# Probabilities times V as one float32 product with the turned probabilities loaded

## The chip, the cores and the metric

The kernel runs on one core of a Trainium2 chip. The metric is the device time of one launch in microseconds (us), the median of several runs. TensorE is written PE below (PEld is its weight load), VectorE is DVE, ScalarE is ACT, GpSimd is POOL and SyncE is SP.

## The reference

One step of a one-layer streaming encoder over 1024 prompt rows and 64 sample rows of width 1024, all in float32:

```
h = rms_norm(x) @ W_in                      # q, k, v of four mixers A, B, C, D, four heads of 64 each
A: stick-breaking weights  w = sigmoid(z) * prod(1 - sigmoid(z of later keys)),   out = w @ v
B: softmax over the own chunk and 2 chunks before, with a sink and a bias,        out = p @ v
C: p = softmax(q1 k1) - lam * softmax(q2 k2), two products with 32 dimensions,    out = rms_norm(p @ v)
D: softmax over the own chunk and 8 chunks before, with a bias,                   out = p @ v
x = x + concat(A, B, C, D) @ W_out
x = x + (silu(rms_norm(x) @ W_gate) * (rms_norm(x) @ W_up)) @ W_down
y = rms_norm(x)                             # and the K and V rows are outputs too
```

The change concerns the four products with v.

## The kernel before

The kernel has three large parts: the projection (up to about 320 us of the profile), the attention (about 325 to 863 us) and the output projection with the feed-forward part (the rest). Float32 products are made as three products of float32r operands: each operand is split into a rounded high part and a low part, and `split_product` (L677 to L679) adds high by high, high by low and low by high in PSUM. In the attention ACT makes the high parts and DVE or POOL the low ones.

The attention runs in rounds, one job each. A job is one score matrix: mixer, block of 128 queries (nine per head, the last one the 64 sample rows) and head; C has two jobs for each block and head. The jobs of one output make a unit: 180 jobs, 144 units, in the order A, B, C, D. The keys of a unit are cut into 1 to 8 blocks of 128, 512 blocks over all units (44 of them with the 64 sample queries). Round r of the loop has, on each engine in this order (all engines run it in parallel, tied by semaphores):

- PE: the scores of job r; `turn_value` of the unit that is 4 rounds old (L846); `turn_probs` of the unit 2 rounds old, one transpose of 128x128 a key block, up to four into one PSUM bank (L813); `values` of the unit 3 rounds old; after the fourth head of a block `turn_out` (L855), which brings the output rows into the layout of the next product.
- ACT: the high parts of q, k and v in the first rounds of a mixer (`high_v`, L1038); the copy of the output of `values` from PSUM to `oT_one` (L1053); the exponential or sigmoid (L1019, L1012); the copies of the turned probabilities to `pt_hi` (L1065).
- DVE: the low parts of v (L1290; for C they are on POOL, L1520) and of q and k; the row maximum (L1234, L1237) or A's scan along the keys (L1248); C's joining of its two matrices (`combine`, L1258); the low parts of the turned probabilities `pt_lo` (L1311); the scaled output rows (`output`, L1272, L1275, L1280).
- POOL: masks and differences of A (L1487, L1495), reciprocals (L1540, L1545), C's split and C's output variance.

`values` multiplies, for each key block, V (64 columns, loaded as the weights) with the turned probabilities (128 queries, streaming), three products a block. Its result is the output turned round, 64x128. So ACT copies it to SBUF, and `turn_value` turns it back on PE before DVE reads it. V must be split before that: each V part's low half takes the place of V in SBUF, so that a mixer's split waits until V has been stored to DRAM (`vrow_out`) and the cached V is in (`vcache_in`).

PE's banks 4 and 5 hold the turned probabilities (and `turn_out`'s result); they come free by `batch_copied`, which DVE raises when the low part is made. Banks 6 and 7 hold the output of `values`.

Of the kernel before, what the change touches and what calls it, by code (L numbers as in the profile page):

```python
# [23 lines left out]
P = 128  # L24
# [73 lines left out]
def build(nc, x_prompt, x_sample, cache_a, cache_b, cache_c, cache_d, norm_attn_g, w_in, w_out,  # L98
# [34 lines left out]
    p_index = {n: i for i, n in enumerate(p_batches)}  # L133

    with ExitStack() as ctx:
# [46 lines left out]
        v_rows_r = sb("v_rows_r", [P, NT, KV_W], F32R, r1r)  # L182
        v_cache_r = sb("v_cache_r", [P, 2, KV_W], F32R, r1r)
# [45 lines left out]
        v_hi = sb("v_hi", [P, NT + 2, 256], F32R, p3)  # L229
        o_rows = sb("o_rows", [P, 2, 256], F32, p3)  # L230
        probs_e = sb("probs_e", [P, 2, D_MODEL], F32, p3)
        oT_one = sb("oT_one", [64, 2, P], F32, p3)
# [23 lines left out]
        pt_hi = [hT_r[:, 14 + s, 0:D_MODEL].rearrange("p (b q) -> p b q", q=P) for s in range(2)]  # L256
        pt_lo = [hT_r[:, 20 + s, 0:D_MODEL].rearrange("p (b q) -> p b q", q=P) for s in range(2)]
# [61 lines left out]
        pt_hi_ready = sem("pt_hi_ready")  # L319
        batch_copied = sem("batch_copied")  # L320
        qk_hi_ready = sem("qk_hi_ready")
        qk_split = sem("qk_split")
        v_hi_ready = sem("v_hi_ready")
        v_split = sem("v_split")
        pv_done = sem("pv_done")
        oT_copied = sem("oT_copied")
        oT_turned = sem("oT_turned")
# [137 lines left out]
        def v_parts(m):  # L465

            w, at = width[m], ROW_OFF[m]
            old = slice(1, 2) if m == "B" else slice(0, 2)
            new = [(v_rows[:, x:y, at:at + w], v_hi[:, x:y, 0:w], v_rows_r[:, x:y, at:at + w])
                   for x, y in ((0, EARLY_BLOCKS), (EARLY_BLOCKS, 5), (5, NT - 1))]  # L470
            return new + [
                    (v_rows[0:DEC, NT - 1, at:at + w], v_hi[0:DEC, NT - 1, 0:w], v_rows_r[0:DEC, NT - 1, at:at + w]),
                    (v_cache[:, old, at:at + w], v_hi[:, NT + old.start:NT + 2, 0:w], v_cache_r[:, old, at:at + w])]

# [12 lines left out]
        V_PARTS, V_EARLY = 5, 1  # L487
        V_ROUND = 2
        def splits_at(r):

            out = []
            for m in "ABCD":
                k = r - first_job[m]
                if k == 0:
                    out.append(("qk", m, 0, QK_EARLY))
                if 1 <= k <= QK_PARTS - QK_EARLY:
                    out.append(("qk", m, QK_EARLY + k - 1, QK_EARLY + k))
                k -= V_ROUND + 1
                if k == 0:
                    out.append(("v", m, 0, V_EARLY))  # L500
                k -= 2
                if 1 <= k <= V_PARTS - V_EARLY:
                    out.append(("v", m, V_EARLY + k - 1, V_EARLY + k))
            return out
# [24 lines left out]
        a_jobs = sum(job.mixer == "A" for job in jobs)  # L529

# [143 lines left out]
        def _(pe):  # L674
# [143 lines left out]
            def values(u):  # L818
# [8 lines left out]
                v_h = slice(job.v_col - ROW_OFF[job.mixer], job.v_col - ROW_OFF[job.mixer] + 64)  # L827
                for t in range(job.blocks):
                    w = job.key_width(t)
                    if t % 4 == 0:  # L830
                        pe.wait_ge(batch_copied, batches[("p", u, t // 4)] + 1)
                    if job.i != SAMPLE:
                        high, low = v_hi[:, job.first + t, v_h], v_rows_r[:, job.first + t, v]
                    elif t < job.past:
                        high, low = v_hi[:, NT + job.first + t, v_h], v_cache_r[:, job.first + t, v]
                    else:
                        high, low = v_hi[0:w, NT - 1, v_h], v_rows_r[0:w, NT - 1, v]
                    mm = split_product(bank(6 + u % 2, job.rows, 64), high, low, pt_hi[u % 2][0:w, t, 0:job.rows],
                                       pt_lo[u % 2][0:w, t, 0:job.rows], t == 0, t == job.blocks - 1)
                mm.then_inc(pv_done, 1)  # L840

            def turn_value(u):

                n = units[u][0].rows
                pe.wait_ge(oT_copied, u + 1)
                pe.transpose(bank(6 + u % 2, 64, n, 256), oT_one[:, u % 2, 0:n], ident[0:64, 0:64])\  # L846
                    .then_inc(oT_turned, 1)

            def turn_out(u):
# [3 lines left out]
                pe.wait_ge(batch_copied, n - 1)  # L853
# [6 lines left out]
            for r in range(rounds):  # L860
                if r < NJ:
                    scores(jobs[r])
                if unit_at(r - NORM_LAG) is not None:
                    turn_value(unit_at(r - NORM_LAG))
# [87 lines left out]
        def _(act):  # L952
# [91 lines left out]
            for r in range(rounds):  # L1044
                for kind, m, at, to in splits_at(r):
                    (high_qk if kind == "qk" else high_v)(m, at, to)
                u = unit_at(r - NORM_LAG)
                if u is not None:
                    n = units[u][0].rows
                    act.wait_ge(pv_done, u + 1)  # L1050
                    if u >= 2:
                        act.wait_ge(oT_turned, u - 1)
                    act.copy(oT_one[:, u % 2, 0:n], bank(6 + u % 2, n, 64)).then_inc(oT_copied, 1)  # L1053
# [5 lines left out]
                if u is not None:  # L1059
                    for b in range(-(-units[u][0].blocks // 4)):  # L1060
# [3 lines left out]
                        for src, to in batch_parts(u, b):  # L1064
                            ins = act.copy(pt_hi[u % 2][to], src)  # L1065
                        ins.then_inc(pt_hi_ready, 1)
                u = unit_at(r - NORM_LAG)
                if u is not None and units[u][0].mixer == "C":
# [3 lines left out]
                    act.wait_ge(oT_turned, u + 1)  # L1072
# [3 lines left out]
                    act.activation(hT[0:n, 9, D_MODEL:D_MODEL + 64], bank(6 + u % 2, 64, n, 256), ACT.Square,  # L1076
# [5 lines left out]
            act.wait_ge(batch_copied, len(batches))  # L1082
# [45 lines left out]
        def _(dve):  # L1128
# [132 lines left out]
            def output(u):  # L1261
# [5 lines left out]
                src = bank(6 + u % 2, 64, n, 256)  # L1267
                if job.head == 0 and u >= 8:
                    dve.wait_ge(batch_ready, batches[("o", u - 5)] + 1)
                if job.mixer == "A":  # L1270
                    dve.wait_ge(oT_turned, u + 1)
# [5 lines left out]
                else:  # L1277
                    dve.wait_ge(inv_ready, inv_count[u])
                    dve.wait_ge(oT_turned, u + 1)
# [151 lines left out]
        def _(pool):  # L1431
# [91 lines left out]
            for u, unit in enumerate(units):  # L1523
                while next_round <= unit[-1].n + 1:
                    for kind, m, at, to in splits_at(next_round):
                        if on_pool(m, at):
                            low_half(kind, m, at)
# [80 lines left out]
```

## Time and profile before

| | us |
|---|---|
| median of 3 runs | 1783.87 |
| the runs | 1776.14, 1783.87, 1784.74 |
| span of the profiled execution | 1776.3 |
| attention in it | about 325 to 863 |

The profile is one execution, and its own time is the span of 1776.3 us between the first and the last instruction; nothing else lies around it. It is as short as the fastest of the three runs and is 7.6 us below their median. "Busy" is the share of time in which an engine has an instruction in hand. PEclk is the granted TensorE clock: 1.00 stands for 2.4 GHz and 0.50 for 1.2 GHz. The ends of matmuls are modelled, since they are pipelined, so how fast PE works is read from one start to the next.

### The profile page before, as it was taken

How to read it: one execution, taken by the hardware profiler on the slowest of the kernel's cores; microseconds unless marked ns; L12 is line 12 of the kernel's file. 1: busy time of each engine (PE TensorE's matmuls, PEld its weight loads, DVE VectorE, ACT ScalarE, POOL GpSimd, SP SyncE). 2: the span in 40 equal slices, each digit the busy share in tenths (PEclk: the TensorE clock that was granted, in tenths of full speed). 3: DMA queues.
4: the chain of work that ended last, by engine and by line, in shares of the span. 5: the costliest groups of instructions: out<-in, count | busy, mean ns of one | idle time of the engine just before them, and what ended most of it. 6: DMA issues, size and time to landing. Idle time of an engine off the chain costs nothing.

```text
span 1776.3 us, 25708 instructions
## 1 busy us (share of the span) xinstructions
PE 1693.1 (95%) x9689; PEld 1511.5 (85%) x9689; DVE 826.3 (47%) x1617; ACT 456.9 (26%) x1160; POOL 259.8 (15%) x437
## 2 busy tenths in 40 slices
PE   5999999799987999999799999999999999999997
PEld 4999999687865777778687899999999999999996
DVE  6111111678665555667722542442543524425425
ACT  4211112545564433455612101001000010010002
POOL 7000000245245322331022100000000000000001
PEclk9999999679575555659899999999999999999999
DMA  7111110400000000010120410111111101111002
GB/s 226 37 47 35 47 47 15 151 1 2 1 1 1 1 0 1 1 72 2 67 82 1 142 48 25 47 47 47 47 44 50 47 24 47 47 47 47 0 0 112
DMA packets 90737, 75.88 MB, mean 43 GB/s; under 512 B 5928, under 2 KB 83273, under 8 KB 90653
## 3 DMA queue, kind: packets, MB, share of 16 engines
q1 hardware_dynamic: 90668, 75.01, 13.7%
q8 instruction: 39, 0.64, 0.1%
q14 instruction: 30, 0.24, 0.0%
HBM read 64.06 MB, written 10.77 MB: 42 GB/s over the span
## 4 chain that ended last, share of the span: by engine, by line
PE 89%; DVE 4%; POOL 3%; ACT 1%; issue 1%; DMA 1%; SPq 1%; ACTq 0%; POOLq 0%; DVEq 0%
PE acc L677 28%; PE acc L678 26%; PE acc L679 26%; PE acc L813 5%; PE acc L846 1%; POOL xlo L1460 1%; PE acc L855 1%; PE acc L759 1%; PE acc L927 1%; PE acc L692 1%; DVE hT_r L1335 1%; DVE hT_r L1311 0%; DVE hT L1248 0%; DVE hT L1258 0%; DMA hT<-in_x_prompt_dram 0%
## 5 line engine op out<-in xcount | busy, mean ns | idle before, releaser
L677 PE MATMUL acc<-ohi,gu_hi 128*128 128x384 f32 (+1 forms) x1056 | 344.3, 326 | 2.8 <-DVE gu_lo L1159 1.9
L679 PE MATMUL acc<-ohi,gu_lo 128*128 128x384 f32 (+1 forms) x1056 | 344.2, 326 | 0.0
L678 PE MATMUL acc<-olo,gu_hi 128*128 128x384 f32 (+1 forms) x1056 | 344.0, 326 | 0.0
L677 PEld LDWEIGHTS acc<-ohi,gu_hi 128*128 128x128 f32 x1056 | 198.2, 188 | 3.8 <-issue 3.3
L678 PEld LDWEIGHTS acc<-olo,gu_hi 128*128 128x128 f32 x1056 | 198.2, 188 | 0.4
L679 PEld LDWEIGHTS acc<-ohi,gu_lo 128*128 128x128 f32 x1056 | 198.2, 188 | 0.0
L1107 ACT ACTIVATE silu<-acc 128x384 f32<-128x384 f32 (+1 forms) x66 | 31.3, 474 | 639.7 <-PE acc L679 638.6
L1384 DVE TENSOR_TENSOR prod<-acc,silu 128x384 f32<-128x384 f32 (+1 forms) x66 | 35.3, 535 | 336.7 <-ACT silu L1107 336.7
L677 PE MATMUL acc<-xhi,win_hi 128*128 128x384 f32 (+1 forms) x528 | 173.1, 328 | 0.0
L679 PE MATMUL acc<-xhi,win_lo 128*128 128x384 f32 (+1 forms) x528 | 172.5, 327 | 0.0
L678 PE MATMUL acc<-xlo,win_hi 128*128 128x384 f32 (+1 forms) x528 | 172.5, 327 | 0.0
L1404 DVE TENSOR_TENSOR x<-acc,x 128x512 f32<-128x512 f32 x198 | 134.4, 689 | 69.1 <-PE acc L679 64.4
L677 PE MATMUL acc<-hT_r,v_hi 128*64 128x128 f32 (+1 forms) x512 | 139.3, 289 | 5.3 <-DVE v_rows_r L1290 2.7
L677 PE MATMUL acc<-k_hi,q_hi 32*128 32x512 f32 (+12 forms) x264 | 129.4, 492 | 12.3 <-DVE hT_r L1285 9.2
L679 PE MATMUL acc<-dn_hi,h_lo 128*128 128x512 f32 x352 | 137.1, 389 | 0.0
L678 PE MATMUL acc<-dn_lo,h_hi 128*128 128x512 f32 x352 | 137.0, 389 | 0.0
L677 PE MATMUL acc<-dn_hi,h_hi 128*128 128x512 f32 x352 | 137.0, 389 | 0.0
L1451 POOL TENSOR_SCALAR meansq<-sumsq 128x1 f32<-128x1 f32 (+1 forms) x27 | 8.9, 329 | 858.4 <-ACT sq_junk L955 767.0
L678 PE MATMUL acc<-hT_r,v_hi 128*64 128x128 f32 (+1 forms) x512 | 126.8, 264 | 0.0
L679 PE MATMUL acc<-hT_r,v_rows_r 128*64 128x128 f32 (+1 forms) x484 | 119.2, 263 | 0.0
L1311 DVE TENSOR_TENSOR hT_r<-acc,hT_r 128x512 fp32r<-128x512 f32 (+4 forms) x208 | 91.8, 466 | 58.2 <-ACT hT_r L1065 57.6
L1065 ACT CAST hT_r<-acc 128x512 fp32r<-128x512 f32 (+4 forms) x208 | 79.3, 412 | 132.5 <-PE acc L813 131.8
(179 smaller groups left out, 3121.4 us busy)
## 6 DMA issues: line engine op xcount, KB each, us to landing
win_raw<-in_w_in_dram SPq DMA_DIRECT2D x22, 512.0 KB, 3.9
ffn_raw<-in_w_gate_dram SPq DMA_DIRECT2D x22, 512.0 KB, 3.8
ffn_raw<-in_w_up_dram SPq DMA_DIRECT2D x22, 512.0 KB, 4.4
ffn_raw<-in_w_down_dram SPq DMA_DIRECT2D x22, 512.0 KB, 4.1
hT<-in_x_prompt_dram SPq DMA_DIRECT2D x8, 512.0 KB, 7.0
hT<-in_w_out_dram SPq DMA_DIRECT2D x8, 512.0 KB, 5.0
x<-in_x_prompt_dram SPq DMA_DIRECT2D x8, 512.0 KB, 5.9
out_dram<-y_out SPq DMA_DIRECT2D x8, 512.0 KB, 2.6
```

Source lines behind the costliest of these rows:

```text
L677: pe.matmul(out, a_hi, b_hi, start=first, stop=False)
L678: pe.matmul(out, a_hi, b_lo, start=False, stop=False)
L679: return pe.matmul(out, a_lo, b_hi, start=False, stop=last)
L692: mm = pe.transpose(bank(base + t % 4, n, at=q * P), xs(j)[0:n, d * P:(d + 1) * P], ident[0:n, 0:n])
L759: mm = pe.transpose(bank(n % 4, P, rows_of(j), t * P), hT[:, tile, j * P:j * P + rows_of(j)], ident[:])
L813: mm = pe.transpose(bank(4 + n % 2, job.rows, w, (t % 4) * P), prob_slot[job.n % 4][0:job.rows, t * P:t * P + w], ident[0:job.rows, 0:job. ...
L846: pe.transpose(bank(6 + u % 2, 64, n, 256), oT_one[:, u % 2, 0:n], ident[0:64, 0:64])\
L1065: ins = act.copy(pt_hi[u % 2][to], src)
L1107: act.activation(silu[:, q % 2, 0:n], bank(2 * (q % 2), n), ACT.Silu).then_inc(silu_done, 1)
L1311: ins = dve.tensor_tensor(pt_lo[u % 2][to], src, pt_hi[u % 2][to].bitcast(F32), ALU.subtract)
L1384: dve.tensor_tensor(prod[:, q % 2, 0:n], bank(2 * (q % 2) + 1, n), silu[:, q % 2, 0:n], ALU.mult).then_inc(prod_done, 1)
L1404: dve.tensor_tensor(part, bank(4 + m % 4), part, ALU.add).then_inc(y_added, 1)
```

## The change

V is no longer split, and the turned probabilities are no longer split. For each key block one float32 product takes their place in which the turned probabilities (128 keys by 128 queries) are the loaded operand and V (64 columns) streams. Its result has queries on the partitions, so the copy to `oT_one` and `turn_value` fall away. Banks 4 and 5 come free when ACT has copied (`pt_copied`), or, after `turn_out`, when DVE has (`o_copied`). SBUF keeps its layout by placeholders. ACT waits at the end of the attention for V's stores; PE waits for the cached V once, at A's sample block.

```diff
-        v_rows_r = sb("v_rows_r", [P, NT, KV_W], F32R, r1r)
-        v_cache_r = sb("v_cache_r", [P, 2, KV_W], F32R, r1r)
+        sb("over_v_rows", [P, NT, KV_W], F32, r1r)
+        sb("over_v_cache", [P, 2, KV_W], F32, r1r)
...
-        pt_hi = [hT_r[:, 14 + s, 0:D_MODEL].rearrange("p (b q) -> p b q", q=P) for s in range(2)]
-        pt_lo = [hT_r[:, 20 + s, 0:D_MODEL].rearrange("p (b q) -> p b q", q=P) for s in range(2)]
+        probs_t = [hT[:, 14 + s, 0:D_MODEL].rearrange("p (b q) -> p b q", q=P) for s in range(2)]
...
+        def wait_batch(eng, n):
+            if n in p_index:
+                eng.wait_ge(pt_copied, p_index[n] + 1)
+            else:
+                eng.wait_ge(o_copied, o_index[n] + 1)
...
             def turn_probs(u):
-                        pe.wait_ge(batch_copied, n - 1)
+                        wait_batch(pe, n - 2)
...
             def values(u):
-                if u == first_unit[job.mixer]:
-                    pe.wait_ge(v_split, V_PARTS * "ABCD".index(job.mixer) + V_EARLY)
-                if job.i >= EARLY_BLOCKS and job.head == 0:
-                    pe.wait_ge(v_split, V_PARTS * ("ABCD".index(job.mixer) + 1))
+                if job.i == SAMPLE and job.head == 0 and job.mixer == "A":
+                    pe.wait_ge(vcache_in, 16 * N_CACHE)
...
-                        pe.wait_ge(batch_copied, batches[("p", u, t // 4)] + 1)
+                        pe.wait_ge(pt_copied, p_index[batches[("p", u, t // 4)]] + 1)
...
-                    mm = split_product(bank(6 + u % 2, job.rows, 64), high, low, pt_hi[u % 2][0:w, t, 0:job.rows],
-                                       pt_lo[u % 2][0:w, t, 0:job.rows], t == 0, t == job.blocks - 1)
+                    mm = pe.matmul(bank(6 + u % 2, 64, job.rows), probs_t[u % 2][0:w, t, 0:job.rows], rows,
+                                   start=t == 0, stop=t == job.blocks - 1)
                 mm.then_inc(pv_done, 1)
-            def turn_value(u):
-                n = units[u][0].rows
-                pe.wait_ge(oT_copied, u + 1)
-                pe.transpose(bank(6 + u % 2, 64, n, 256), oT_one[:, u % 2, 0:n], ident[0:64, 0:64])\
-                    .then_inc(oT_turned, 1)
...
-            def high_v(m, at, to):
-                if at == 0:
-                    if m != "A":
-                        act.wait_ge(pv_done, first_unit[m])
-                    act.wait_ge(vrow_out[m], 16 * sum(kv_target(m, j) is not None for j in range(NT)))
-                    act.wait_ge(vcache_in, 16 * N_CACHE)
-                for src, high, _ in v_parts(m)[at:to]:
-                    act.copy(high, src).then_inc(v_hi_ready, 1)
...
-                    act.copy(oT_one[:, u % 2, 0:n], bank(6 + u % 2, n, 64)).then_inc(oT_copied, 1)
...
-                            ins = act.copy(pt_hi[u % 2][to], src)
-                        ins.then_inc(pt_hi_ready, 1)
+                            ins = act.copy(probs_t[u % 2][to], src)
+                        ins.then_inc(pt_copied, 1)
...
-                    act.wait_ge(oT_turned, u + 1)
+                    act.wait_ge(pv_done, u + 1)
...
-            act.wait_ge(batch_copied, len(batches))
+            act.wait_ge(o_copied, len(o_batches))
+            for m in "ABCD":
+                act.wait_ge(vrow_out[m], 16 * sum(kv_target(m, j) is not None for j in range(NT)))
...
-                src = bank(6 + u % 2, 64, n, 256)
+                src = bank(6 + u % 2, 64, n)
...
-            def low_v(m, at, to):
-                for i, (src, high, low) in enumerate(v_parts(m)[at:to], at):
-                    dve.wait_ge(v_hi_ready, V_PARTS * "ABCD".index(m) + i + 1)
-                    dve.tensor_tensor(low, src, high.bitcast(F32), ALU.subtract).then_inc(v_split, 1)
...
-                    for b in range(-(-units[u][0].blocks // 4)):
-                        dve.wait_ge(pt_hi_ready, p_index[batches[("p", u, b)]] + 1)
-                        for src, to in batch_parts(u, b):
-                            ins = dve.tensor_tensor(pt_lo[u % 2][to], src, pt_hi[u % 2][to].bitcast(F32), ALU.subtract)
-                        ins.then_inc(batch_copied, 1)
```

## Rows read from the trace of the kernel before

**Rows 1.** The page: engines, and the granted clock in 40 slices.
```profile
PE 1693.1 (95%) x9689; PEld 1511.5 (85%) x9689; DVE 826.3 (47%) x1617; ACT 456.9 (26%) x1160; POOL 259.8 (15%) x437
...
PEclk9999999679575555659899999999999999999999
```

**Rows 2.** The page: the chain that ended last, by engine.
```profile
PE 89%; DVE 4%; POOL 3%; ACT 1%; issue 1%; DMA 1%; SPq 1%; ACTq 0%; POOLq 0%; DVEq 0%
```

**Rows 3.** Windows: stretch, length, PE, PEld, DVE, ACT, POOL busy, PEclk.
```profile
325.80:377.00 51.20, 45.03 (x209) 35.64 (x210) 31.92 (x60) 23.99 (x58) 17.94 (x33) 0.50 0.25 74
377.00:441.80 64.80, 60.66 (x597) 52.69 (x595) 58.76 (x82) 35.09 (x79) 37.11 (x38) 1.00 0.00 1
441.80:493.10 51.30, 50.02 (x271) 41.60 (x271) 33.64 (x131) 28.22 (x99) 13.01 (x22) 0.50 0.01 1
...
545.00:687.60 142.60, 140.39 (x577) 104.17 (x577) 80.08 (x205) 57.62 (x184) 42.40 (x111) 0.50 0.00 1
687.60:757.00 69.40, 64.97 (x372) 51.02 (x372) 45.89 (x104) 33.17 (x95) 19.45 (x50) 0.65 0.00 1
...
800.20:858.30 58.10, 55.89 (x546) 49.32 (x546) 43.56 (x143) 35.25 (x104) 11.49 (x21) 1.00 0.01 2
```

**Rows 4.** The page: the costliest groups, first product with V.
```profile
L677 PE MATMUL acc<-hT_r,v_hi 128*64 128x128 f32 (+1 forms) x512 | 139.3, 289 | 5.3 <-DVE v_rows_r L1290 2.7
```

**Rows 5.** Windows: instructions with v_hi alone (two products a block).
```profile
377.00:441.80 64.80, 24.17 (x230) 21.81 (x230) 0.00 (x0) 0.00 (x0) 0.00 (x0) 1.00 0.00 1
...
800.20:858.30 58.10, 21.58 (x196) 18.88 (x196) 0.00 (x0) 0.00 (x0) 0.00 (x0) 1.00 0.01 2
```

**Rows 6.** Windows: instructions with oT_one alone (PE, PEld, ACT).
```profile
377.00:441.80 64.80, 4.53 (x18) 2.45 (x18) 4.88 (x19) 1.00 0.00 1
...
800.20:858.30 58.10, 5.54 (x22) 2.94 (x22) 5.61 (x22) 1.00 0.01 2
```

**Rows 7.** Timeline of PE (start, duration) at 1.2 GHz: V, 12 steps apart.
```profile
641.64 0.31 PE L679 MATMUL acc<-hT_r,v_rows_r 128*64 128x128 f32 x1
...
642.92 0.31 PE L679 MATMUL acc<-hT_r,v_rows_r 128*64 128x128 f32 x1
```

**Rows 8.** Timeline of PE at 2.4 GHz: V, 16 steps apart.
```profile
399.58 0.23 PE L678 MATMUL acc<-hT_r,v_hi 128*64 128x128 f32 x1
...
400.54 0.22 PE L679 MATMUL acc<-hT_r,v_rows_r 128*64 128x128 f32 x1
```

**Rows 9.** Timeline of PE at 1.2 GHz: scores, 128 columns loaded, 128 streaming.
```profile
522.01 0.41 PE L678 MATMUL acc<-hT_r,q_hi 32*128 32x128 f32 x1
522.23 0.41 PE L679 MATMUL acc<-k_hi,hT_r 32*128 32x128 f32 x1
```

**Rows 10.** Source line L729, true float32 products: durations, first and last start.
```profile
L729 PE MATMUL acc<-hT x12: 590/592/592, 62.7 to 67.4; 128*128 128x512 f32 x12
```

**Rows 11.** Timeline of PE at 1.2 GHz: turn_value, transposes behind it.
```profile
645.37 0.36 PE L846 MATMUL acc<-ident,oT_one 64*128 64x64 f32 x1
645.67 1.54 PE L813 MATMUL acc<-ident,hT 128*128 128x128 f32 x6
```

**Rows 12.** Waits, 325 to 377 us: total, times, longest.
```profile
PE acc L677 <- DVE v_rows_r L1290: 2.7, 1, 2.7
```

**Rows 13.** Waits, 515 to 545 us.
```profile
PE acc L813 <- DVE hT L1258: 7.1, 2, 4.5
```

**Rows 14.** Timeline of POOL: a split of C's V (two of this size).
```profile
533.39 1.81 POOL L1520 TENSOR_TENSOR v_rows_r<-v_rows,v_hi 128x768 fp32r<-128x768 f32 x1
```

**Rows 15.** Windows: DVE's line L1311 alone.
```profile
377.00:441.80 64.80, 18.71 (x37) 1.00 0.00 1
```

**Rows 16.** Windows in C: before and in a spell at 2.4 GHz.
```profile
684.20:687.60 3.40, 3.40 (x26) 2.75 (x24) 1.66 (x4) 0.22 (x2) 1.17 (x3) 0.50 0.02 5
687.60:691.00 3.40, 3.40 (x18) 2.55 (x18) 3.14 (x6) 2.00 (x6) 0.00 (x0) 1.00 0.00 0
```

**Rows 17.** Windows: instructions with v_hi alone, before that spell.
```profile
684.20:687.60 3.40, 2.40 (x14) 2.21 (x14) 0.00 (x0) 0.00 (x0) 0.00 (x0) 0.50 0.02 5
```

More of the change, by code:

```diff
@@ L133, in build @@
     p_index = {n: i for i, n in enumerate(p_batches)}
+    o_batches = [n for key, n in sorted(batches.items(), key=lambda kv: kv[1]) if key[0] == "o"]
+    o_index = {n: i for i, n in enumerate(o_batches)}
     with ExitStack() as ctx:
@@ L494, in splits_at @@
                 if k == 0:
-                    out.append(("qk", m, 0, QK_EARLY))
+                    out.append((m, 0, QK_EARLY))
                 if 1 <= k <= QK_PARTS - QK_EARLY:
[L497 to L503, printed above, removed]
+                    out.append((m, QK_EARLY + k - 1, QK_EARLY + k))
             return out
@@ L830, in values @@
                     if t % 4 == 0:
-                        pe.wait_ge(batch_copied, batches[("p", u, t // 4)] + 1)
[L832 to L835, printed above, removed]
-                    else:
-                        high, low = v_hi[0:w, NT - 1, v_h], v_rows_r[0:w, NT - 1, v]
-                    mm = split_product(bank(6 + u % 2, job.rows, 64), high, low, pt_hi[u % 2][0:w, t, 0:job.rows],
-                                       pt_lo[u % 2][0:w, t, 0:job.rows], t == 0, t == job.blocks - 1)
+                        pe.wait_ge(pt_copied, p_index[batches[("p", u, t // 4)]] + 1)
+                    if job.i == SAMPLE and t < job.past:
+                        rows = v_cache[0:w, job.first + t, v]
+                    elif job.i == SAMPLE:
+                        rows = v_rows[0:w, NT - 1, v]
+                    else:
+                        rows = v_rows[0:w, job.first + t, v]
+                    mm = pe.matmul(bank(6 + u % 2, 64, job.rows), probs_t[u % 2][0:w, t, 0:job.rows], rows,
+                                   start=t == 0, stop=t == job.blocks - 1)
                 mm.then_inc(pv_done, 1)
-            def turn_value(u):
-                n = units[u][0].rows
-                pe.wait_ge(oT_copied, u + 1)
-                pe.transpose(bank(6 + u % 2, 64, n, 256), oT_one[:, u % 2, 0:n], ident[0:64, 0:64])\
-                    .then_inc(oT_turned, 1)
             def turn_out(u):
@@ L1044, in _ @@
             for r in range(rounds):
[L1045 to L1052, printed above, removed]
-                    act.copy(oT_one[:, u % 2, 0:n], bank(6 + u % 2, n, 64)).then_inc(oT_copied, 1)
+                for m, at, to in splits_at(r):
+                    high_qk(m, at, to)
                 if r < NJ and jobs[r].mixer == "A":
@@ L1075, in _ @@
                         act.wait_ge(c_factor, k)
-                    act.activation(hT[0:n, 9, D_MODEL:D_MODEL + 64], bank(6 + u % 2, 64, n, 256), ACT.Square,
+                    act.activation(hT[0:n, 9, D_MODEL:D_MODEL + 64], bank(6 + u % 2, 64, n), ACT.Square,
                                    scale=row_inv[0:n, job.n:job.n + 1], accum_out=c_var[0:n, 1:2])\
@@ L1510, in output_root, with low_qk @@
                     .then_inc(c_factor, 1)
-            def low_half(kind, m, part):
-                parts, per_mixer, ready, done = ((qk_parts(m), QK_PARTS, qk_hi_ready, qk_split) if kind == "qk"
-                                                 else (v_parts(m), V_PARTS, v_hi_ready, v_split))
-                src, high, low = parts[part]
-                count = per_mixer * "ABCD".index(m) + part
-                pool.wait_ge(done, count)
-                pool.wait_ge(ready, count + 1)
-                pool.tensor_tensor(low, src, high.bitcast(F32), ALU.subtract).then_inc(done, 1)
+            def low_qk(m, part):
+                src, high, low = qk_parts(m)[part]
+                count = QK_PARTS * "ABCD".index(m) + part
+                pool.wait_ge(qk_split, count)
+                pool.wait_ge(qk_hi_ready, count + 1)
+                pool.tensor_tensor(low, src, high.bitcast(F32), ALU.subtract).then_inc(qk_split, 1)
             next_round = 0
@@ L1524, in _ @@
                 while next_round <= unit[-1].n + 1:
-                    for kind, m, at, to in splits_at(next_round):
+                    for m, at, to in splits_at(next_round):
                         if on_pool(m, at):
-                            low_half(kind, m, at)
+                            low_qk(m, at)
                     next_round += 1
```

37 lines of the change are left out of this document (8 added, 29 removed).

## The prediction

> **What bounds the kernel now.** The page comes first: PE is busy for 95% of the span, and 89% of the chain that ended last is PE [rows 1, 2]. The change leaves the projection and the feed-forward part alone, so I cut the attention into stretches wherever the granted clock changes and read the busy times there [rows 3]. The reader is to see two kinds of stretch. At 1.2 GHz PE has nearly no pause: 140.4 of 142.6 us in C, 50.0 of 51.3 in B. There one step of PE more is one step of time more. At 2.4 GHz (A from 377 to 441.8, D from 800.2 to 858.3) PE is busy too, but in A DVE is busy for 58.8 of 64.8 us and the two wait for each other. The page's PEclk digits of 5 to 7 say that most of the attention runs at 1.2 GHz [rows 1]. What follows is therefore costed at either level, by the step from one start to the next, because durations of pipelined matmuls overlap.
>
> **Products with V.** Each of the 512 blocks [rows 4] now has three instructions, each loading 64 columns and streaming 128. Twelve steps take 1.28 us at 1.2 GHz, 0.107 each, so a block costs 0.32 us [rows 7]; at 2.4 GHz sixteen take 0.96, 0.060 each, 0.18 us a block [rows 8].
>
> The new product is true float32. The bias flips are such products: six in the code are 12 instructions in the trace, each 0.427 us after the last ((67.4 - 62.7)/11) for 512 streaming columns at 2.4 GHz [rows 10]. That is two instructions a product, and each column streams twice. So a new block is two instructions, each loading 128 columns and streaming 64. Streaming takes twice 64 columns, 0.107 us at 1.2 GHz. Loading is longer: where 128 columns are loaded for 128 that stream, the step is 0.22 us, twice the 0.107 that streaming them needs [rows 9]. I take exactly twice, 0.213. A block is then 2 x 0.213 = 0.427 us at 1.2 GHz and half of that, 0.214, at 2.4: 0.107 and 0.034 us more than now. This takes it that a load lies wholly behind the product before it, as in [rows 9]. If it didn't, an instruction would cost 0.213 + 0.107 and a block 0.64; if the load cost nothing, a block would be 0.214. I take 0.427, since the row has the same load size.
>
> The Trainium skill, page "TensorE: Matmul & The Clock Gate", section "LDWEIGHTS (loading the stationary operand)", gives a load as its columns divided by 1.2 in ns, which is 0.107 us for 128 columns at either clock. By that a new block would cost 0.214 at 1.2 GHz and the change would save about 0.1 us on each block there. The row says 0.213 a load, and the row decides.
>
> How many at which clock: at two instructions a block [rows 5], 115 blocks in A's fast stretch and 98 in D's run at 2.4 GHz; I put the other 299 at 1.2 (some in B and C are faster, at a price near the same). Of the 512, 44 have 64 queries; loading 64 columns only, they gain about 0.107 us each at 1.2 GHz instead, and 32 of them are there. Sum: 267 x 0.107 - 32 x 0.107 = +25 us, and at 2.4 GHz 201 x 0.034, less 12 x 0.05, = +6. Together **+31 us**.
>
> **The second turn.** `turn_value` takes 0.30 us of PE at 1.2 GHz before the transposes behind it can start [rows 11], and half of that at 2.4. 40 of 144 are in the fast stretches [rows 6]. Removed: 104 x 0.30 + 40 x 0.15 = 37 us. Seven of the slow ones lie between 513 and 545 us, where PE stands waiting anyway, so **-35 us**. The ACT copies to `oT_one` (4.9 us in A's stretch) go as well; ACT has room everywhere (35.1 of 64.8), so that is worth nothing by itself.
>
> So PE's own work changes by -4 us: the turn pays for the loads.
>
> **Waits that go.** At A's start the first product waits 2.7 us for V's low part [rows 12], and the high part before it was held back by the cached V and V's stores; without them PE starts its values as soon as they are turned: -4. At C's start PE waits 7.1 us for DVE's joining [rows 13]; that waits for POOL's reciprocals, and in POOL's queue between them stand the splits of V, two of 1.8 us and two shorter ones [rows 14]. The splits of q and k stay there and take the same places, so I count -4, the two of 1.8, and not the whole 7. In A's fast stretch DVE loses L1311, 18.7 of its 58.8 us [rows 15], and is no longer close to the bound; PE is, at 61 of 65. I count -4, from the few pauses it has. In the slow stretches L1311 and V's splits are hidden behind PE now, and dropping them yields nothing. The bank of the turned probabilities comes free one DVE instruction sooner, which shortens nothing PE waits for in C. New waits: PE waits once for the cached V at A's last block, which A's first product with V already waits for now, so it is free. ACT waits for V's stores after the last product; SP stored them hundreds of us before. Total of the waits **-12**.
>
> With the clock as it is: 1776.3 - 16 = 1760 for the profiled execution, and 1783.9 - 16 = 1768 for the median, of which the profiled span is 7.6 us short.
>
> **The clock.** This is the large unknown. In C PE is at 1.2 GHz although it pauses for only 2.2 of 142.6 us [rows 3]. Its first rise follows a stretch that products with V fill for 2.4 of 3.4 us, and lasts for the next stretch, without such products [rows 16, 17]. From 687.6 to 757 the mean clock is 0.65 [rows 3], so (0.65 - 0.50)/0.50 x 69.4, about 20 us of it, are at 2.4 GHz in a few spells of this kind. The new product leaves the array streaming for only half of its time, the load taking the rest; so I expect some of these spells to go. All of them gone: 20 us of work at half the speed, less the quarter in which PE paused, +15. I take half, **+8**.
>
> **Forecast:** 1783.9 - 16 + 8 = **1776 us**, its own range 1760 to 1792 (all or none of the spells, and 8 for the waits). Chance 0.55.
>
> **Rivals.**
>
> *The clock of A, B and D falls too* (slower). What speaks for it: C shows that PE without pause can stay at 1.2, and half of A's products with full use of the array go. Against: A's fast stretch holds over 65 us, also where DVE holds PE up. Price: in A's fast stretch a unit has 6.5 blocks on average; at 1.2 GHz its scores are 832 x 3 columns, 2.1 us, transposes 6.5 x 0.213 = 1.4, products 6.5 x 0.427 = 2.8, and 0.4 between them: 6.7 us, for 18 units 120 us against 64.8. D's 20 units of 5 blocks at 5.6 us make 111 against 58. With B's 20 us it is +115: 1768 + 115 = 1883, or 1898 with C's spells gone. It decides from about a tenth of those stretches on. Chance 0.27, most of it between 1820 and 1898, since one stretch can fall alone.
>
> *The clock rises in C* (much faster). PE's pauses shorten, which speaks for it; C staying at 1.2 with next to none speaks against. At 2.4 GHz PE's 140 us become 70, and then DVE's 80 less its lows (about 16) and the chain of ACT and DVE would bound: about 87, -55, and -10 in the rest of C: 1703. The page named above lays a low clock to pauses between bursts of matmuls (section "Why this matters for your kernels"); by that rule the clock would be kept or rise. The stretches of C do not agree with it [rows 3]. Chance 0.10.
>
> *Loads are not hidden:* 0.64 us a block, +0.32 x 267 + 0.14 x 201 = +113, less the 35 and 12 above and a few for the 64-query blocks: 1784 + 113 - 47 = about 1850. The row of the loads speaks against [rows 9]. Chance 0.05. Other ways 0.03.
>
> **How the numbers follow.** The measurement can tell about 0.5% from no change, 1775 to 1793. Of the forecast's 0.55, 0.26 ends below, 0.25 within and 0.04 above; the rise in C adds 0.10 below, and the other cases, 0.35, are above. So faster 0.36, same 0.25, slower 0.39. The range leaves out the far end of the fall (over 1885, 0.10) and most of the rise in C (under 1755, 0.10): 1755 to 1885.
>
> **What would show it.** Right: products with V as 1024 instructions, 0.21 us apart at 1.2 GHz and 0.107 at 2.4; no L846; A's PEclk 1.00 from about 375 us; DVE at 40 of A's 60 us. Wrong: steps of 0.32 (loads in the open) or 0.11 (loads cheaper than in rows 9, -50 us); PEclk 0.50 all through A or D; C at 1.00 anywhere for longer than 10 us; and a wait of PE on ACT's copy of the turned probabilities at C's start as long as the 7.1 before.

## The result, and the profile after

The changed kernel takes 1895.5 us (median of 4 runs, 1886.0 to 1896.6), the kernel before 1784.1 beside it (4 runs, 1776.1 to 1784.7): ratio 1.064, interval 1.059 to 1.069. It is slower by 111 us; the forecast said 1776 and 1755 to 1885. The price of the first rival, 1883 to 1898, is what was measured. Some executions run a few per cent longer at a lower granted clock; ratios and intervals here leave those out, medians and ranges don't.

The page of the profile after (engines, the granted clock in 40 slices, the chain that ended last by engine) answers to [rows 1, 2]:

```profile
span 1893.5 us, 23855 instructions
PE 1826.1 (96%) x9033; PEld 1632.6 (86%) x9033; DVE 744.7 (39%) x1393; ACT 417.2 (22%) x996; POOL 249.3 (13%) x433
...
PEclk8999999555555555555559999999999999999999
...
PE 92%; POOL 3%; DVE 2%; issue 1%; ACT 1%; DMA 1%; SPq 0%; ACTq 0%; POOLq 0%; DVEq 0%
```

PE has 656 instructions fewer than before and is busy 133 us longer. The digits tell why: slices 8 to 21 are all 5, where before there were 6, 7, 8 and 9 among them. The records of the clock say the same: from 324.0 to 993.0 us, all through the attention, the granted clock is 0.50, 1.2 GHz. The windows of the attention stretches, with the same columns as [rows 3], show that PE doesn't pause more than before (over the attention it is busy for 628.9 of 652 us, before for 497.4 of 534):

```profile
377.00:441.80 64.80, 64.80 (x245) 56.23 (x244) 32.66 (x23) 17.24 (x31) 18.33 (x21) 0.50 0.00 1
441.80:530.00 88.20, 86.20 (x370) 74.41 (x369) 39.43 (x99) 32.54 (x88) 24.07 (x33) 0.50 0.00 1
530.00:800.00 270.00, 257.75 (x894) 200.56 (x892) 113.85 (x332) 98.37 (x302) 77.82 (x175) 0.50 0.00 1
800.00:960.00 160.00, 155.50 (x619) 133.03 (x620) 55.64 (x189) 54.81 (x162) 30.67 (x63) 0.50 0.05 20
```

From 377 us on, where PE had gone over to 2.4 GHz in [rows 3], it is now busy for all of 64.8 us at 1.2 GHz.

Cut at the first exponential or sigmoid of each mixer, and at D's last exponential, which can be found in both traces:

| stretch | before, us | of it at 2.4 GHz | after, us | of it at 2.4 GHz | difference |
|---|---|---|---|---|---|
| A | 119.8 | 64.9 | 169.6 | 0 | +49.8 |
| B | 70.5 | 20.5 | 82.4 | 0 | +11.8 |
| C | 241.1 | 20.5 | 253.0 | 0 | +11.9 |
| D | 98.2 | 56.3 | 143.5 | 0 | +45.3 |

That is 118.8 us; the spans (1893.5 and 1776.3) are 117.2 apart, the rest of the kernel being 1.6 shorter. What the change did to the work can be read where both kernels run at 1.2 GHz: from A's job 0 to job 16, and from C's job 72 to job 124. Windows of these stretches, before (the first two) and after:

```profile
517.20:687.50 170.30, 155.58 (x640) 115.25 (x639) 92.30 (x238) 69.41 (x227) 62.88 (x134) 0.50 0.00 1
326.90:372.80 45.90, 39.96 (x182) 31.30 (x181) 29.82 (x55) 21.67 (x54) 16.65 (x31) 0.50 0.25 76
```
```profile
578.30:744.30 166.00, 155.25 (x510) 118.22 (x509) 72.06 (x201) 61.14 (x195) 57.19 (x130) 0.50 0.00 1
326.40:370.60 44.20, 40.09 (x141) 31.48 (x142) 25.45 (x36) 15.98 (x37) 17.06 (x31) 0.50 0.27 78
```

170.3 us became 166.0 and 45.9 became 44.2. At an equal clock the work got a little cheaper, as forecast, so the loss is put down to the clock; the experiments test that.

### The profile page after: what moved, and what is told of

The parts are those of the page before. It is cut to its first block, busy times and chain, and to the rows that moved or that the text cites. A ratio compares the mean times of both kernels' runs of the same rounds, so it can differ in the third digit from the quotient of the medians.

```text
span 1893.5 us, 23855 instructions
## 1 busy us (share of the span) xinstructions
PE 1826.1 (96%) x9033; PEld 1632.6 (86%) x9033; DVE 744.7 (39%) x1393; ACT 417.2 (22%) x996; POOL 249.3 (13%) x433
## 4 chain that ended last, share of the span: by engine, by line
PE 92%; POOL 3%; DVE 2%; issue 1%; ACT 1%; DMA 1%; SPq 0%; ACTq 0%; POOLq 0%; DVEq 0%
PE acc L659 25%; PE acc L661 23%; PE acc L660 23%; PE acc L817 11%; PE acc L795 7%; PE acc L827 1%; POOL xlo L1404 1%; PE acc L897 1%; PE acc L674 0%; DVE hT_r L1279 0%; PE acc L741 0%; DVE hT_r L1241 0%; POOL c_var L1449 0%; DVE olo L1275 0%; DMA hT<-in_x_prompt_dram 0%
## 5 line engine op out<-in xcount | busy, mean ns | idle before, releaser
L817 PEld LDWEIGHTS acc<-v_rows,hT 128*128 128x128 f32 (+1 forms) x968 | 218.1, 327 | 15.2 <-issue 6.6
L817 PE MATMUL acc<-v_rows,hT 128*128 128x64 f32 (+1 forms) x968 | 225.8, 410 | 1.2 <-DVE o_rows L1231 1.2
L659 PE MATMUL acc<-k_hi,q_hi 32*128 32x512 f32 (+12 forms) x264 | 149.8, 569 | 10.2 <-DVE hT_r L1241 7.8
L1019 ACT COPY hT<-acc 128x512 f32<-128x512 f32 (+4 forms) x208 | 80.3, 410 | 250.5 <-PE acc L795 249.6
L661 PE MATMUL acc<-k_hi,hT_r 32*128 32x512 f32 (+12 forms) x264 | 127.4, 486 | 0.0
L659 PEld LDWEIGHTS acc<-k_hi,q_hi 64*128 64x128 f32 (+3 forms) x264 | 74.2, 282 | 51.0 <-issue 23.7
```

The lines of the kernel that those rows point to most:

```text
L659: pe.matmul(out, a_hi, b_hi, start=first, stop=False)
L661: return pe.matmul(out, a_lo, b_hi, start=False, stop=last)
L817: mm = pe.matmul(bank(6 + u % 2, 64, job.rows), probs_t[u % 2][0:w, t, 0:job.rows], rows, start=t == 0, stop=t == job.blocks - 1)
L1019: ins = act.copy(probs_t[u % 2][to], src)
```

## The experiments

The theory: the products with V now stream 64 columns for every 128 loaded, and that takes the clock from PE. The rivals: something else of the change costs the time (the instructions' number, the removed turn, waits), or the clock falls only because PE has less or more to do. The kernel before was run again beside each group of experiments (medians 1784.7 to 1800.8 us), and each ratio is to those runs.

**V streams 128 columns.** The neighbouring head's V streams along and its result is not read.

```diff
-                v = slice(job.v_col, job.v_col + 64)
+                v = slice(job.v_col - 64 * (job.v_col // 64 % 2), job.v_col - 64 * (job.v_col // 64 % 2) + 128)
...
-                    mm = pe.matmul(bank(6 + u % 2, 64, job.rows), probs_t[u % 2][0:w, t, 0:job.rows], rows,
+                    mm = pe.matmul(bank(6 + u % 2, 128, job.rows), probs_t[u % 2][0:w, t, 0:job.rows], rows,
```

> The changed kernel with V streaming 128 columns instead of 64 for each loaded block of probabilities; the 64 columns of the neighbouring head are computed and not used. Streaming 128 columns twice takes 0.213 us at 1.2 GHz, as long as the load of 128 columns, so that PE's work at an equal clock stays what it is. Theory (the 111 us are the clock: the same work at 1.2 GHz, because the loads leave the array without streaming columns): A and D go back to 2.4 GHz for most of their time, steps of 0.107 us there, 1760 to 1790 us. Rival 1 (loading the probabilities, or a wait of the new order, costs the time): no change, 1890 to 1900, or more if streaming adds to the load. Rival 2 (the clock falls because of float32 products or of the missing turn, not of idle columns): PEclk stays 0.50, 1890 to 1900.

Measured: 1756.0 us (1753.8 to 1761.3), ratio to before 0.984, interval 0.974 to 0.993. The trace has the same 23855 instructions as the changed kernel. The timeline of PE at 1.2 GHz, first the changed kernel, then this one:

```profile
705.79 2.82 PE L817 MATMUL acc<-v_rows,hT 128*128 128x64 f32 x12
```
```profile
564.84 2.08 PE L817 MATMUL acc<-v_rows,hT 128*128 128x128 f32 x8
```

A row is the time from the first start to the last end. A last instruction in it takes 0.42 us in both, so the steps are at most (2.82 - 0.42)/11 = 0.22 and (2.08 - 0.42)/7 = 0.24, with a longer first one in each row; the median from one start to the next is 0.213 us in both kernels. The columns that were added are free at 1.2 GHz, as forecast from the load of 128 columns, which sets the step. With the same steps at the same clock the kernel is 139 us faster, and its windows show where from:

```profile
358.00:436.60 78.60, 75.95 (x538) 64.82 (x538) 65.00 (x61) 35.31 (x71) 39.70 (x46) 1.00 0.00 1
436.60:457.00 20.40, 20.40 (x79) 15.05 (x79) 11.85 (x47) 10.95 (x34) 7.14 (x10) 0.50 0.00 1
457.00:498.00 41.00, 39.41 (x277) 31.56 (x275) 23.88 (x119) 26.49 (x92) 14.88 (x28) 1.00 0.01 1
503.00:638.00 135.00, 126.14 (x403) 94.08 (x404) 59.62 (x170) 49.27 (x161) 46.47 (x111) 0.50 0.00 1
...
778.00:839.00 61.00, 60.18 (x440) 52.21 (x440) 29.06 (x106) 30.98 (x82) 10.93 (x20) 1.00 0.01 1
```

A, B and D are at 2.4 GHz again (78.5, 40.6 and 56.3 us), A and B for longer than before the change and D for as long. So neither the removed turn nor the waits cost anything; this version keeps all of the change but the width of what streams.

**The old roles in float32.** V is loaded (64 columns), the turned probabilities stream (128 columns), and the copy to `oT_one` and `turn_value` are back; V and the probabilities stay unsplit.

```diff
-                    mm = pe.matmul(bank(6 + u % 2, 64, job.rows), probs_t[u % 2][0:w, t, 0:job.rows], rows,
+                    mm = pe.matmul(bank(6 + u % 2, job.rows, 64), rows, probs_t[u % 2][0:w, t, 0:job.rows],
...
+            def turn_value(u):
+                pe.wait_ge(oT_copied, u + 1)
+                pe.transpose(bank(6 + u % 2, 64, n, 256), oT_one[:, u % 2, 0:n], ident[0:64, 0:64])\
+                    .then_inc(oT_turned, 1)
...
```

> The changed kernel with the roles of before: V is loaded (64 columns), the turned probabilities stream (128), still one float32 product and no splits; the copy to oT_one and turn_value are back. A block is two instructions of 128 columns streamed twice, 0.427 us at 1.2 GHz, as in the changed kernel; the turn adds 0.30 a unit, 35 us in all. Theory (clock, through columns that don't stream): A and D at 2.4 GHz again, 1784 + 31 for the products - 12 for the waits = about 1803, less if C rises too. Rival (work): 1895 + 35 = 1930.

Measured: 1802.0 us (1791.9 to 1813.1), ratio 1.008, interval 1.003 to 1.014. A was at 2.4 GHz for 81.9 us, C for 51.2, D for 57.6. True float32 as such doesn't take the clock; loading the wide operand and streaming the narrow one does.

**Halves.** Each product is made of two, with 64 queries each: 64 columns loaded, 64 streaming.

```diff
-                    mm = pe.matmul(bank(6 + u % 2, 64, job.rows), probs_t[u % 2][0:w, t, 0:job.rows], rows,
-                                   start=t == 0, stop=t == job.blocks - 1)
+                    for q in range(0, job.rows, 64):
+                        out = acc[q:q + 64, (6 + u % 2) * 512:(6 + u % 2) * 512 + 64]
+                        mm = pe.matmul(out, probs_t[u % 2][0:w, t, q:q + 64], rows,
+                                       start=t == 0, stop=t == job.blocks - 1)
```

> The changed kernel with each block's product cut into two of 64 queries: four instructions, each loading 64 columns (0.107 us at 1.2 GHz) and streaming V's 64 twice (0.107), 0.427 a block as now. Theory (clock): the array streams all the time with 64 of its 128 columns; if streaming time is what counts, A and D are back at 2.4 GHz and it takes 1760 to 1790; if only half of the array's columns doesn't do, 1890 to 1900 with PEclk 0.50. Rival (work): 1895, and above it if the 64-column steps are longer than 0.107.

Measured: 1789.9 us (1773.1 to 1804.2), ratio 1.000, interval 0.995 to 1.006. This looks like the clock brought back, but it isn't the test that I meant it to be, since the work didn't stay the same. The expectation had 0.427 us a block; the trace shows two blocks of 128 queries, eight instructions, in one row at 1.2 GHz:

```profile
562.54 0.69 PE L819 MATMUL acc<-v_rows,hT 128*64 128x64 f32 x8
```

An instruction alone is 0.31 us long. The two products of a block write to different halves of the partitions; they start 0.007 us apart, and the next pairs follow 0.107 us apart, so the two run beside each other. A block costs about 0.21 us, half of what it costs in the changed kernel. C shows it without the clock: at 1.2 GHz throughout in both profiled executions, it takes 227.7 us where it took 253.0. By an estimate from these steps (0.213 us less in each of 468 blocks of 128 queries), up to 100 of the 106 us can be cheaper work. With less work than the kernel with 128 columns it is still slower (its fastest execution took 1773.1 us, that kernel's longest 1761.3), so it keeps less of the clock; how much it keeps isn't shown.

**Filler.** Two extra products a unit, 4 columns loaded and 128 streaming, whose result is overwritten. If streaming anything often enough kept the clock, this would.

```diff
+                for k in range(2):
+                    pe.matmul(bank(6 + u % 2, P, 4, 256), ident[:, 0:4], ident[:], start=True, stop=True)
```

> The changed kernel with two products more in each of the 144 units, whose result nobody reads: 4 columns of the identity loaded, its 128 streaming, float32, 0.85 us a unit at 1.2 GHz and 0.43 at 2.4. Theory (clock): more work, yet A and D rise to 2.4 GHz: 1895 - 95 + 31 there and + 61 in B and C, about 1890. Rival (work): 1895 + 144 x 0.85 = 2017.

Measured: 2016.8 us (2008.7 to 2017.3), ratio 1.127, interval 1.116 to 1.138: what the rival had said, 2017. The extra work was paid in full and more (a unit's four instructions take 0.95 us at 1.2 GHz, not 0.85), and only 37.7 us of the attention, in A, ran at 2.4 GHz. My theory missed here as I had put it: streaming alone isn't enough. PE was busy throughout, too, and without the clock:

```profile
350.00:466.00 116.00, 116.00 (x420) 84.17 (x420) 48.02 (x45) 26.82 (x48) 27.64 (x38) 0.50 0.00 1
504.40:630.00 125.60, 125.05 (x492) 80.15 (x492) 36.22 (x163) 35.13 (x124) 22.34 (x37) 0.50 0.00 1
```

**Filler with 128 columns loaded.** The same two products a unit with the whole of `ident` loaded instead of 4 columns of it.

```diff
-                    pe.matmul(bank(6 + u % 2, P, 4, 256), ident[:, 0:4], ident[:], start=True, stop=True)
+                    pe.matmul(bank(6 + u % 2, P, P, 256), ident[:], ident[:], start=True, stop=True)
```

> As filler, but the two products more load all 128 columns of the identity in place of 4; same time, 0.85 us a unit at 1.2 GHz and 0.43 at 2.4. If the loaded width counts too (filler rose to 2.4 GHz only from 467 to 504 us): A and D at 2.4 GHz for most of their time, about 1895 - 95 + 31 + 61 = 1890. If only the time of streaming counts: 2017, as filler.

Measured: 1904.6 us (1891.4 to 1912.2), ratio 1.066, interval 1.055 to 1.078: 112 us less than with 4 columns, with the same count of instructions (24866) and the same columns streaming. A has 61.4 us and D 61.1 us at 2.4 GHz. Not all of the 112 us is the clock: B and C, where neither filler has a rise, are shorter by 11.6 and 2.0 us. The windows of this kernel around its first rise:

```profile
350.00:407.00 57.00, 57.00 (x222) 49.23 (x221) 23.16 (x24) 14.26 (x27) 15.21 (x24) 0.50 0.00 0
407.30:468.80 61.50, 59.99 (x455) 53.38 (x454) 46.05 (x39) 24.83 (x49) 26.76 (x31) 1.00 0.01 1
```

So how many of the array's columns are loaded while something streams matters as well.

**V streams 96 columns**, half of the neighbouring head with the own one (`V_OWN` is 0 or 32, where the own head begins among them).

```diff
-                v = slice(job.v_col, job.v_col + 64)
+                v = slice(job.v_col - V_OWN(job), job.v_col - V_OWN(job) + 96)
...
-                    mm = pe.matmul(bank(6 + u % 2, 64, job.rows), probs_t[u % 2][0:w, t, 0:job.rows], rows,
+                    mm = pe.matmul(bank(6 + u % 2, 96, job.rows), probs_t[u % 2][0:w, t, 0:job.rows], rows,
```

> As wide128, but V streams 96 columns. The load (0.213 us at 1.2 GHz) still sets the step, the array streams for three quarters of it. Theory (the clock follows how long the array streams): part of A and D at 2.4 GHz, between 1756 and 1895, say 1800. If it is on or off: 1756 or 1895.

Measured: 1805.2 us (1804.2 to 1829.3, 5 runs), ratio 1.012, interval 1.002 to 1.022; the profiled run is the long one of 1829. It lies between 64 columns and 128 in time and, in that run, in clock: A 54.6, B 0, C 13.7 and D 29.9 us at 2.4 GHz.

**The kernel before with a wide load.** Nothing of the change: three products of rounded parts, but each loads 128 columns of V, the neighbouring head's with the own. They stream 128 columns once, 0.107 us at 1.2 GHz [rows 7], in a step that the load makes 0.213.

```diff
-                v = slice(job.v_col, job.v_col + 64)
-                v_h = slice(job.v_col - ROW_OFF[job.mixer], job.v_col - ROW_OFF[job.mixer] + 64)
+                v_at = job.v_col // 128 * 128
+                v = slice(v_at, v_at + 128)
+                v_h = slice(v_at - ROW_OFF[job.mixer], v_at - ROW_OFF[job.mixer] + 128)
...
-                    mm = split_product(bank(6 + u % 2, job.rows, 64), high, low, pt_hi[u % 2][0:w, t, 0:job.rows],
+                    mm = split_product(bank(6 + u % 2, job.rows, 128), high, low, pt_hi[u % 2][0:w, t, 0:job.rows],
```

> The kernel before with each V load made 128 columns (the neighbouring head's V too; its rows of the result are not used). Three products a block, the load sets each step, 0.213 us at 1.2 GHz and 0.107 at 2.4, so a block costs 0.64 or 0.32 us in place of 0.32 or 0.18, and the array streams for half of it. By the steps alone, with the clock as before: + 299 x 0.32 + 213 x 0.14 = + 125, about 1910. Theory (long loads take the clock): A and D at 1.2 GHz too, another 100 to 150, about 2030. Rival (the clock fell because of float32 products, not of loads): 1910 and A and D at 2.4 GHz.

Measured: 2030.8 us (2019.4 to 2031.8), ratio 1.136, interval 1.124 to 1.147, and from 324.3 to 1129.8 us the clock never rose. Of the 246 us more, the expectation had put 125 to the longer steps by themselves; the rest is the loss of the changed kernel made in the other one, with none of its float32 products, exchanged roles or missing turn:

```profile
377.00:441.80 64.80, 64.80 (x263) 57.89 (x263) 25.62 (x38) 17.23 (x36) 14.24 (x18) 0.50 0.00 1
...
850.00:1100.00 250.00, 245.66 (x1010) 214.26 (x1010) 109.66 (x303) 84.31 (x244) 38.43 (x81) 0.50 0.04 13
```

**128 columns in A alone**, 64 in the others: is the clock set by what runs at that moment? `V_FIRST` gives the first column of V and their number.

```diff
+        def V_FIRST(job):
+            if job.mixer == "A":
+                return job.v_col // 128 * 128, 128
+            return job.v_col, 64
...
```

> V streams 128 columns in A alone (the head's own 64 and its neighbour's, unused), 64 in B, C and D as in the changed kernel. If the clock is set by the products that run at that moment, A takes some 112 us as in the kernel with 128 columns everywhere (169.6 with 64), D stays at 1.2 GHz near 143 us, and B lies between 59 and 82: 1895 - 58 = 1837 us, down to 1815 with B's clock. If one fall anywhere keeps the clock down or one rise keeps it up, D changes too: 1756 to 1795, or 1895.

Measured: 1845.5 us (1840.7 to 1845.6), ratio 1.030, interval 1.018 to 1.041. A took 117.1 us, 71.7 of them at 2.4 GHz, B 83.8, C 253.1 and D 143.6 as in the changed kernel (82.4, 253.0, 143.5). The clock was local: it rose in A and was gone with A's end.

```profile
370.20:441.80 71.60, 69.09 (x499) 59.58 (x497) 57.13 (x52) 32.53 (x66) 35.90 (x41) 1.00 0.00 1
803.00:923.00 120.00, 120.00 (x480) 105.32 (x479) 33.05 (x120) 34.66 (x94) 13.71 (x25) 0.50 0.00 1
```

A gained 52.5 us where I had said 58, since it rose 12 us later than in the kernel with 128 columns everywhere; so 1845 and not 1837.

**More than the load asks for, in C.** 128 columns in A, B and D; in C 256, the V of all four of its heads, and in a second kernel 192.

```diff
+        def V_FIRST(job):
+            if job.mixer == "C":
+                return ROW_OFF["C"], 256
+            return job.v_col // 128 * 128, 128
...
```

> As wide128, with V streaming 256 columns (all four heads, three unused) in C's 156 blocks alone. An instruction then takes 0.427 us at 1.2 GHz and 0.213 at 2.4. If C's clock stays: 1756 + 156 x 0.427 = about 1822. If C rises to 2.4 GHz for most of its 240 us, its scores and transposes take half: 1756 + 156 x 0.43 / 2 - 100 + what DVE and ACT then hold back, 1690 to 1740.

> V streams 128 columns in A, B and D and 192 in C (128 of them of no use). If C's clock rises as with 256 columns (136 of its 208 us at 2.4 GHz), its blocks of 192 columns cost 0.32 us at 2.4 GHz instead of 0.427, and the time is a little below that of 256: 1710 to 1735 us. If 192 don't bring the clock up, the third more of streaming is paid at 1.2 GHz, 0.32 instead of 0.213 us a product instruction: 1756 + up to 40 = 1756 to 1796 us.

Measured with 256: 1731.7 us (1729.6 to 1738.9), ratio 0.971, interval 0.962 to 0.981. With 192: 1732.6 us (1730.8 to 1734.1), ratio 0.967, interval 0.956 to 0.978. Both beat the kernel before and the changed one (by 164 and 163 us). C's time went from 235.8 us with 128 columns to 208.4 and 208.2, with 136.5 and 102.4 us of it at 2.4 GHz. In C the added columns are not free, as the timeline of the first one at 2.4 GHz shows:

```profile
650.91 0.33 PE L669 MATMUL acc<-k_hi,hT_r 32*128 32x384 f32 x1
651.18 1.99 PE L826 MATMUL acc<-v_rows,hT 128*128 128x256 f32 x8
```

About 0.22 us a step, against 0.112 for 128 columns. In this stretch the doubled streaming is paid at the doubled clock, and everything else in C gets the clock for nothing:

```profile
608.80:704.40 95.60, 94.71 (x473) 72.11 (x472) 53.65 (x119) 45.06 (x118) 27.62 (x72) 1.00 0.00 1
```

Between 192 and 256 no difference was measured: 192 has the cheaper step, 256 the longer spells. Against 128 columns everywhere the ratios to the kernel before (0.984, and 0.971 and 0.967) have intervals that overlap a little; that the gain is C's is read from the traces (235.8 to 208.4 and 208.2).

What the kernels' products with V look like (192 and 256 stand for C, with 128 in the other mixers), with the time that each spent at 2.4 GHz between 326 us and its last exponential (a float32 instruction streams its columns twice, one of rounded parts once):

| kernel | loaded x streaming | step at 1.2 GHz, us | at 2.4 GHz, us | time, us |
|---|---|---|---|---|
| wide load in the kernel before | 128 x 128, once | 0.213 | 0 | 2030.8 |
| changed kernel | 128 x 64, twice | 0.213 | 0 | 1895.5 |
| 96 columns | 128 x 96, twice | 0.213 | 98 | 1805.2 |
| 128 columns | 128 x 128, twice | 0.213 | 206 | 1756.0 |
| 192 in C | 128 x 192, twice | 0.320 | 268 | 1732.6 |
| 256 in C | 128 x 256, twice | 0.427 | 309 | 1731.7 |
| kernel before | 64 x 128, once | 0.107 | 162 | 1784.1 |
| old roles, float32 | 64 x 128, twice | 0.213 | 191 | 1802.0 |

## Why the prediction was wrong

**The step that failed is the clock,** and in it the sentence "I take half, +8", with the forecast's premise that A, B and D keep theirs. I had named the cause, "the new product leaves the array streaming for only half of its time, the load taking the rest", and applied it to C's spells only, 20 us, where all of them gone was put at +15; the same products are in A, B and D, which had 142 us at 2.4 GHz to lose. What I set against the fall was that "A's fast stretch holds over 65 us, also where DVE holds PE up". That was the weak reason: in that stretch the products with V streamed through the whole of their step [rows 5, 8], and just this was changed. What the runs showed in its place: no spell at 2.4 GHz from 324.0 to 993.0 us, +118.8 us over the four mixers for the +8 of the forecast. The kernel with the wide load in the old products, 0 us at 2.4 GHz, shows that the rest of A doesn't hold the clock beside such products.

**The rival's price was right.** It put A's fast stretch at 120 us for 64.8 (+55) and D's at 111 for 58 (+53), which leaves 7 of its +115 for B, and C's spells at +15. Measured by mixer, A, D, B, C: +49.8, +45.3, +11.8, +11.9, in which the savings, forecast at 16 us, are contained. Its total is nearer than its parts, and that is partly luck: D's 5.6 us a unit is more than the terms used for A give for 5 blocks (scores 1.6, transposes 1.07, products 2.13, between them 0.4, so 5.2 and +46 in D), and B was short by 5. The rival had been given a chance of 0.27.

**The price of a block was right at 1.2 GHz.** 1024 instructions in 512 blocks; the source line's groups in the changed kernel are

```profile
L817 PE MATMUL acc<-v_rows,hT x968: 311/421/477, 331.6 to 979.6; 128*128 128x64 f32 x188, 64*64 64x64 f32 x6
...
L817 PE MATMUL acc<-v_cache,hT x56: 314/314/369, 489.2 to 979.2; 128*64 128x64 f32 x56
```

and the starts at 1.2 GHz are 0.213 us apart (median). With 128 columns at 2.4 GHz they are 0.112, where I had 0.107. The rival with loads in the open is out, and so is a load of 0.107 us at 1.2 GHz. The Trainium skill, "TensorE: Matmul & The Clock Gate", section "LDWEIGHTS (loading the stationary operand)", would have made the step 0.107; the trace doesn't agree.

**The turn and the sum.** In C from job 72 to 124 there are 184 of the new instructions, 92 blocks, of which 88 have 128 queries: 88 x 0.107 = +9.4, the other four -0.4, and 27 turns at 0.30 make -8.1. With the wait at C's start forecast at -4 that is -3.1; measured -4.3. The waits of PE in these stretches, before and after, answer to [rows 13]:

```profile
PE acc L813 <- DVE hT L1258: 8.3, 4, 4.5
PE acc L813 <- DVE probs_e L1258: 5.1, 2, 2.8
```
```profile
PE acc L795 <- DVE hT L1214: 7.0, 4, 3.2
PE acc L795 <- DVE probs_e L1214: 3.3, 2, 2.5
```

13.4 us became 10.3, so 3.1 of the 4 came. At A's start I had 4 from the waits for V's parts; those are gone, but the stretch of jobs 0 to 16 became shorter by only 1.7. There the 56 new instructions stand for 28 blocks, +3.0, and 13 turns for -3.9, so the waits gave about 0.8.

**DVE in A** was to be busy for 40 of 60 us. In the kernel with 128 streaming columns it is busy for 65.0 of 78.6. L1311 is gone, but the scans have grown. Timeline of DVE before, and of DVE and POOL in the kernel with 128 columns, for scans of the same size (POOL's line, L1495 before, takes the differences of A's weights):

```profile
394.80 2.19 DVE L1248 TENSOR_TENSOR_SCAN hT<-probs_e 128x768 f32<-128x768 f32 x1
```
```profile
385.35 3.04 DVE L1204 TENSOR_TENSOR_SCAN hT<-probs_e 128x768 f32<-128x768 f32 x1
```
```profile
385.31 1.46 POOL L1439 TENSOR_TENSOR probs_x<-hT 128x768 f32<-128x768 f32 x1
```

Before, L1311 stood ahead of the scan, and most of POOL's difference (from 393.92 to 395.38) was over when the scan began at 394.80: 0.58 us beside each other. Now both start together, 1.42 us beside each other, and the scan is longer by 0.85. POOL's difference is 1.46 us in both. With nothing of POOL's beside it the same scan takes 1.75:

```profile
388.71 1.75 DVE L1248 TENSOR_TENSOR_SCAN hT<-hT 128x768 f32<-128x768 f32 x1
```

It is DVE that pays. The Trainium skill, "SBUF — State Buffer", section "Who interferes with whom", has DVE and GpSimd share a pair of ports as an exclusive lock; the three durations agree with a scan that stands still for nearly all of the time that POOL's difference runs beside it: 0.44 us longer for 0.58, 1.29 for 1.42. PE is busy for 75.95 of the 78.6 us there, so this probably hid behind PE; no run tests it.

**A rise in C** was a rival at 0.10, and it fell with the change as made. It came with 192 or 256 columns streaming, and C gained 33 us on the kernel before (241.1 to 208.4), not 65. The rule that a low clock comes from pauses (the Trainium skill, "TensorE: Matmul & The Clock Gate", section "Why this matters for your kernels") is contradicted more widely than by [rows 3]: 64.8 of 64.8 us busy at 1.2 GHz in the changed kernel, 116.0 of 116.0 with the filler.

**What stays open.** Which quantity the chip goes by isn't settled. How much of the time the array streams puts the six kernels that load 128 columns in the table's order, as far as they differ in it; the two fillers show that the width loaded counts too, and the kernel before holds the clock with 64 columns loaded. One quantity that fits both families wasn't looked for. Why C got so little of the clock before the change (20.5 of 241.1 us) and with 128 columns (31.1 of 235.8) wasn't tested either; its scores fill 32 of the array's 128 rows [rows 9], which may be the reason.

## What to carry to other kernels

When two operands of a matmul are exchanged, price both the step and how much of the step the array streams: here the step at 1.2 GHz was forecast at 0.213 us and came out so, and the clock that it cost was worth far more than the work that it saved. If the load sets the step, stream up to as many columns as fit under it, even useless ones: 64 more columns cost no longer step and gave 139 us. And a premise by which one stretch loses its clock has to be applied to every stretch that has the same products. Before an experiment is read as showing the clock, check in its trace that the work stayed the same: the halves' didn't.

## What was not expected of the hardware

- PE without any pause (116.0 of 116.0 us, 64.8 of 64.8) stayed at the lower of its two clocks, and went to the higher one at the same count of instructions when the products streamed 128 columns for 64.
- Adding useless work made C faster: 256 columns for 128, at twice the price a step, took it from 235.8 to 208.4 us (the kernel from 1756.0 to 1731.7).
- Of two fillers with the same instructions and streaming columns, the one that loads 128 columns for 4 was 112 us faster.
- Two float32 products that load 64 columns each and write to different halves of the partitions start 0.007 us apart: a block cut so cost 0.21 us for 0.427 at 1.2 GHz.
- A scan on DVE grew from 1.75 to 2.19 and 3.04 us with 0, 0.58 and 1.42 us of a POOL instruction beside it, while that instruction stayed at 1.46. Taking L1311 off DVE, 27.8 us in A, moved the scans beside POOL's differences, and A's 36 scans grew from 52.4 to 69.6 us: 17 of the 28 were taken back.
